# A second attention whose values run one pair later, whose pair shares a bank, and whose first scores move among the query panels

## What is computed

```python
s = jnp.einsum('bnqhgd,bnkhd->bnhgqk', qb, kw) * (HEAD_DIM_2 ** -0.5)
s = s - slopes[:, :, None, None] * dist.astype(jnp.float32)
s = jnp.where(mask[None, :, None, None], s, -jnp.inf)
m = jnp.maximum(jnp.max(s, axis=-1, keepdims=True), sink)
p = jnp.exp(s - m)
denom = jnp.sum(p, axis=-1, keepdims=True) + jnp.exp(sink - m)
o = jnp.einsum('bnhgqk,bnkhd->bnqhgd', p / denom, vw)
return o.reshape(B, T, ATTN_Q_DIM) @ w_out
```

## Time and profile before

| what | us |
|---|---|
| median of 3 runs | 2631.68 |
| lowest and highest | 2622.22, 2632.99 |
| the profiled execution's own time | 2619.79 |
| its span, first to last instruction | 2618.0 |
| TensorE matmuls busy in the span | 2490.8 (95%) |
| VectorE busy | 1694.2 (65%) |
| ScalarE busy | 931.9 (36%) |
| last query panel's last matmul to the first `SO` matmul (line 468) | 2096.98 to 2183.29 |

### The profile page before, as it was taken

The page is one execution under the profiler, slowest core; times in us unless marked ns, Lnnn a source line. Parts: engine busy times, 40 slices in busy tenths (PEclk is TensorE's granted clock), DMA queues, the critical chain, the costliest instruction groups (busy, mean ns, idle before and its releaser), DMA issues.

```text
span 2618.0 us, 34786 instructions
## 1 busy us (share of the span) xinstructions
PE 2490.8 (95%) x11828; PEld 2090.1 (80%) x11828; DVE 1694.2 (65%) x3166; ACT 931.9 (36%) x1315; POOL 739.6 (28%) x646
## 2 busy tenths in 40 slices
PE   8999999998999999999989899999999968999998
PEld 4877877686887887887778799999999746788786
DVE  5887768688666667676712377888888574444334
ACT  4223852623233333333222333333334473222222
POOL 0000000000025666676664256777730000000000
PEclk9999999998999999999999899999999988999999
DMA  6223813354234444444354489999996201222221
GB/s 248 97 73 116 311 48 121 115 190 153 81 125 141 137 141 137 148 142 137 129 184 158 159 290 329 364 365 362 360 366 217 89 9 57 89 96 96 88 96 64
DMA packets 177219, 433.56 MB, mean 166 GB/s; under 512 B 32752, under 2 KB 81904, under 8 KB 176752
## 3 DMA queue, kind: packets, MB, share of 16 engines
q1 hardware_dynamic: 123888, 331.61, 36.9%
q0 software_dynamic: 34816, 67.41, 7.3%
q10 hardware_dynamic: 18432, 33.56, 3.4%
HBM read 371.48 MB, written 61.01 MB: 165 GB/s over the span
## 4 chain that ended last, share of the span: by engine, by line
PE 82%; DVE 8%; ACT 4%; another core or an unknown queue 3%; issue 2%; ACTq 0%; DMA 0%; DVEq 0%; SPq 0%
PE ps L468 16%; PE ps L470 15%; PE ps L469 15%; PE ps L793 8%; PE ps L795 8%; PE ps L794 8%; DVE wlo L1372 2%; PE ps L706 2%; DVE ar L1425 1%; PE ps L690 1%; PE ps L538 1%; ACT whi L924 1%; PE ps L698 1%; ACT ar L1285 1%
## 5 line engine op out<-in xcount | busy, mean ns | idle before, releaser
L1372 DVE TENSOR_TENSOR wlo<-raw,whi 128x1024 fp32r<-128x1024 f32 x426 | 521.4, 1224 | 625.2 <-ACT whi L924 540.2
L2192 POOL DMA_INDIRECT w_scratch<-ar x384 | 416.8, 1085 | 986.6 <-DVE wlo L1372 881.0
L924 ACT ACTIVATE whi<-raw 128x1024 fp32r<-128x1024 f32 x424 | 448.9, 1059 | 687.6 <-PE ps L795 363.7
L468 PE MATMUL ps<-b_hi,whi 128*128 128x512 f32 x1328 | 524.4, 395 | 26.7 <-DVE wlo L1372 18.3
L470 PE MATMUL ps<-b_hi,wlo 128*128 128x512 f32 x1328 | 521.1, 392 | 0.2 <-issue 0.2
L469 PE MATMUL ps<-b_lo,whi 128*128 128x512 f32 x1328 | 521.2, 392 | 0.0
L793 PE MATMUL ps<-a_hi,whi 128*128 128x384 f32 x1024 | 347.6, 339 | 13.1 <-DVE a_lo L1949 11.0
L794 PE MATMUL ps<-a_lo,whi 128*128 128x384 f32 x1024 | 346.4, 338 | 0.4 <-issue 0.4
L795 PE MATMUL ps<-a_hi,wlo 128*128 128x384 f32 x1024 | 346.2, 338 | 0.4 <-issue 0.4
L468 PE MATMUL ps<-a_hi,whi 128*128 128x512 f32 x816 | 325.5, 399 | 8.9 <-DVE wlo L1372 7.2
L468 PEld LDWEIGHTS ps<-b_hi,whi 128*128 128x128 f32 x1328 | 251.7, 190 | 86.1 <-DVE wlo L1372 24.1
(11 more groups left out here) (273 smaller groups left out, 3039.1 us busy)
## 6 DMA issues: line engine op xcount, KB each, us to landing
raw<-panels SPq DMA_DIRECT2D x430, 512.0 KB
gelu_scratch<-ar ACTq DMA_DIRECT2D x128, 256.0 KB
w_scratch<-rstd SPq DMA_DIRECT2D x32, 768.0 KB, 11.1
ar<-w_scratch SPq DMA_DIRECT2D x128, 192.0 KB
ar<-gelu_scratch SPq DMA_DIRECT2D x128, 192.0 KB
ar<-mod SPq DMA_DIRECT2D x32, 512.0 KB, 5.2
ar<-panels SPq DMA_DIRECT2D x3, 2048.0 KB, 20.4
w_scratch<-ar POOLq DMA_INDIRECT x384
```

The source lines that it names most:

```text
L468: pe.matmul(bank, w_h, hi[:, k, :], start=(k == 0), stop=False)
L924: act.activation(whi[:, u % SPLIT, :], raw[:, u % RAW, :], ACT.Copy).then_inc(hi_ready, 1)
L1372: dve.tensor_tensor(wlo[:, u % SPLIT, :], raw[:, u % RAW, :], f32(whi[:, u % SPLIT, :]), ALU.subtract).then_inc(lo_ready, 1)
L2192: nc.gpsimd.indirect_dma_start(experts, bass.IndirectOffsetOnAxis(offs[:, k:k + 1], 0), vals[:, k:k + 1], None)\
```

## The change

- `swa_values(m)` is issued after the first transpose step of pair m + 1 and before its second. The last pair's values come after both of its own.
- A pair's two halves of the values go to one bank, 2 + m % 2, each on its own 64 partitions. `swa_hi` and `swa_lo` take a whole pair, 128 partitions at a time: 8 of each where there were 16.
- The banks change place: scores in 4 to 7, transposes in 0 and 1, values in 2 and 3.
- `swa_scores(0)` is issued after the sixth query panel. VectorE runs `swa_bias(0)` and `swa_bias(1)` after the seventh query panel, before the eighth.
- ScalarE's order for a pair is out, exp, hi, out, exp. VectorE's is norm, norm, bias, bias (of pair m + 2), lo.
- `s2` has 6 groups, `p2T` 3. `rstd1` and the bias tables are moved in the arena; `tiny` grows to 96 columns.
- The first `SO` panel waits for 7 of the 8 pairs, and for the eighth after its fourth step.

The core of the difference (swa_bias and swa_norm are the same but for `n % 6` and the banks):

```diff
-        s2 = area(A_S2, 4, 1024)
+        s2 = area(A_S2, 6, 1024)
-        p2T = area(A_PT2, 4, 512)
+        p2T = area(A_PT2, 6, 512)
...
             def swa_values(m):
...
                 pe.wait_ge(ptc2, 2 * m + 2)
-                if m:
-                    pe.wait_ge(o2, 2 * m)
-                else:
-                    pe.wait_ge(rt_ready, 5)
+                if m >= 2:
+                    pe.wait_ge(o2, m - 1)
                 for s in tiles:
                     for half in range(2):
                         rows_ = slice(half * HD2, (half + 1) * HD2)
                         kv = 2 * kt + half
-                        last = pe.matmul(ps[rows_, 6 + half, :], v2[:, b - 1 + s, kv * HD2:(kv + 1) * HD2], p2T[:, 2 * half + s, :],
+                        last = pe.matmul(ps[rows_, 2 + m % 2, :], v2[:, b - 1 + s, kv * HD2:(kv + 1) * HD2],
+                                         p2T[:, 2 * ((2 * m + half) % 3) + s, :],
                                          start=(s == tiles[0]), stop=(s == 1))
...
+            def early_scores(i, u):
...
+                if not (isinstance(i, int) and i == 0) and u == 1:
+                    pe.wait_ge(v2_done, 2)
+                    pe.wait_ge(rt_ready, 5)
+                    pe.wait_ge(bank_free, r_of(SW + 4) + 8)
+                    swa_scores(0)
+
+            strips(SW + 4, 8, a_hi, a_lo, early_scores, banks=SWB)
+            pe.wait_ge(bank_free, r_of(SO) + 4)
             swa_scores(1)
             for m in range(len(groups) // 2):
                 if m + 2 < len(groups) // 2:
                     swa_scores(m + 2)
                 swa_turn(2 * m)
+                if m:
+                    swa_values(m - 1)
                 swa_turn(2 * m + 1)
-                swa_values(m)
-
-            pe.wait_ge(o2, len(groups))
-            strips(SO, KT, b_hi, b_lo)
+            swa_values(len(groups) // 2 - 1)
+
+            def last_outputs(k):
+                if k == KT // 2 - 1:
+                    pe.wait_ge(o2, len(groups) // 2)
+
+            pe.wait_ge(o2, len(groups) // 2 - 1)
+            strips(SO, KT, b_hi, b_lo, each=last_outputs)
...
             swa_exp(0)
             swa_exp(1)
-            for n in range(0, len(groups), 2):
-                for c in range(2):
-                    if n + 2 < len(groups):
-                        swa_exp(n + 2 + c)
-                    if n:
-                        swa_hi(n - 2 + c)
-                swa_out(n)
-                swa_out(n + 1)
-            swa_hi(len(groups) - 2)
-            swa_hi(len(groups) - 1)
+            for m in range(len(groups) // 2):
+                more = 2 * m + 2 < len(groups)
+                swa_out(2 * m)
+                if more:
+                    swa_exp(2 * m + 2)
+                if m:
+                    swa_hi(m - 1)
+                swa_out(2 * m + 1)
+                if more:
+                    swa_exp(2 * m + 3)
+            swa_hi(len(groups) // 2 - 1)
...
+                if n == 6:
+                    dve.wait_ge(bias_ready, NH2 // 2)
+                    swa_bias(0)
+                    swa_bias(1)
+
             dve.wait_ge(bias_ready, NH2)
-            dve.wait_ge(bank_free, r_of(SO) + 4)
-            swa_bias(0)
-            swa_bias(1)
-            for n in range(0, len(groups), 2):
...
+            swa_bias(2)
+            swa_bias(3)
+            for m in range(len(groups) // 2):
+                swa_norm(2 * m)
+                swa_norm(2 * m + 1)
+                if m + 2 < len(groups) // 2:
+                    swa_bias(2 * m + 4)
+                    swa_bias(2 * m + 5)
+                if m:
+                    swa_lo(m - 1)
+            swa_lo(len(groups) // 2 - 1)
```

More of the change, by code:

```diff
@@ L496, in two_panels, with strips, four @@
                         tile(1, s - LAG)
-            def strips(first, count, hi, lo, after=None, ready=None, banks=(0, 1, 2, 3), two=False):
-                def four(i, ready=None):
+            def strips(first, count, hi, lo, after=None, ready=None, banks=(0, 1, 2, 3), two=False, each=None):
+                def four(i, ready=None, each=None):
                     for u in range(4):
                         if not (ready and two and u < 2):
-                            panel(i * 4 + (first + u), u, ps[:, banks[u], :], hi, lo, i * 4 + (r_of(first) + u + 1), ready if u == 0 else None)
+                            panel(i * 4 + (first + u), u, ps[:, banks[u], :], hi, lo, i * 4 + (r_of(first) + u + 1), ready if u == 0 else None,
+                                  each if u == 0 else None)
                         elif u == 0:
@@ L510, in four @@
                         after(i, 4)
-                four(0, ready)
+                four(0, ready, each)
                 if count > 4:
@@ L832, in _ @@
                 last.then_inc(v2_turned, 1)
[L833 to L842, removed]
             groups = [(b, kt, half) for b in range(TT) for kt in range(2) for half in range(2)]
@@ L865, in swa_turn @@
                     for r in range(4):
-                        last = pe.transpose(ps[:, 4 + s, r * P:(r + 1) * P], s2[:, n % 4, r * 256 + s * P:r * 256 + (s + 1) * P], ident)
+                        last = pe.transpose(ps[:, s, r * P:(r + 1) * P], s2[:, n % 6, r * 256 + s * P:r * 256 + (s + 1) * P], ident)
                 last.then_inc(pt2, 1)
@@ L2020, in _, with swa_bias @@
                 dve.tensor_copy(v2[:, :, u * P:(u + 1) * P], ps[:, 4 + u, :].rearrange("p (s n) -> p s n", n=P)).then_inc(v2_done, 1)
+            groups = [(b, kt, half) for b in range(TT) for kt in range(2) for half in range(2)]
+            def swa_bias(n):
+                b, kt, half = groups[n]
+                o = 16 * (n % 6)
+                dve.wait_ge(sc2, n // 2 + 1)
+                if n >= 6:
+                    dve.wait_ge(pt2, n - 5)
+                for r in range(4):
+                    h = 8 * kt + 4 * half + r
+                    at = P if b == 0 else 0
+                    dve.tensor_tensor_reduce(s2[:, n % 6, r * 256 + at:(r + 1) * 256],
+                                             ps[:, 4 + 2 * half + r // 2, (r % 2) * 256 + at:(r % 2) * 256 + 256],
+                                             bias[:, h, at:256], 1.0, -3.0e38, ALU.add, ALU.max, tiny[:, o + r:o + r + 1]).then_inc(bias2, 1)
+                dve.wait_ge(bias2, 4 * (n + 1))
+                h = 8 * kt + 4 * half
+                dve.tensor_tensor(tiny[:, o:o + 4], tiny[:, o:o + 4], col("sinks", h, 4), ALU.max).then_inc(mx2, 1)
+                dve.wait_ge(mx2, n + 1)
+                dve.tensor_scalar(tiny[:, o + 4:o + 8], tiny[:, o:o + 4], -1.0, None, ALU.mult).then_inc(nmx2, 1)
+                dve.tensor_tensor(tiny[:, o + 12:o + 16], col("sinks", h, 4), tiny[:, o:o + 4], ALU.subtract).then_inc(nmx2, 1)
@@ new lines, in swa_norm @@
+            def swa_norm(n):
+                o = 16 * (n % 6)
+                dve.wait_ge(e2, 4 * (n + 1))
+                dve.wait_ge(snk2, n + 1)
+                dve.tensor_tensor(tiny[:, o + 8:o + 12], tiny[:, o + 8:o + 12], tiny[:, o + 12:o + 16], ALU.add).then_inc(den2, 1)
+                dve.wait_ge(den2, n + 1)
+                dve.reciprocal(tiny[:, o + 12:o + 16], tiny[:, o + 8:o + 12]).then_inc(rec2, 1)
+                dve.wait_ge(rec2, n + 1)
+                at = P if groups[n][0] == 0 else 0
+                pr = s2[:, n % 6, :].rearrange("p (r n) -> p r n", r=4)[:, :, at:256]
+                dve.tensor_tensor(pr, pr, tiny[:, o + 12:o + 16].unsqueeze(2).to_broadcast([P, 4, 256 - at]), ALU.mult).then_inc(pn2, 1)
@@ L2021, in _, with swa_lo @@
+            def swa_lo(m):
+                b, kt, half = groups[2 * m]
+                dve.wait_ge(ohi2, m + 1)
+                at = slice(b * P, (b + 1) * P)
+                dve.tensor_tensor(b_lo[:, kt * 4:kt * 4 + 4, at], ps[:, 2 + m % 2, :].rearrange("p (r t) -> p r t", r=4),
+                                  f32(b_hi[:, kt * 4:kt * 4 + 4, at]), ALU.subtract).then_inc(o2, 1)
             for n in range(8):
```

88 lines of the change are left out of this document (19 added, 69 removed).

## The result

The changed kernel takes 2607.9 us (median of 4 runs, 2598.1 to 2610.7); the kernel before 2632.3 (4 runs, 2622.2 to 2634.8). The ratio is 0.9911 with a 95% interval of 0.9887 to 0.9934: 23 us less (24 by the medians), and between 17 and 30. A second set, taken with the experiments, gave 2607.1 against 2632.4, 0.9901 (0.9870 to 0.9933).

What follows compares the result with a forecast made beforehand. TensorE, with matmuls in 95% of the span, was taken as the bound, its idle time in second attention (85.9 us) the target. Pairs 11.0, head 1.9 and tail 2.1 sum to 15.0 us, giving 2616.7 us, range 2606 to 2627.

Steps and rivals of the forecast that it cites:

- The pairs: Second attention, first transpose of pair 0 to that of pair 7: 63.3 us falls to 52.3, gain 11.0.
- The loop of two pairs: Second attention, a loop through TensorE, ScalarE and VectorE: 15.95 us for two pairs, 8.0 a pair.
- The head: End of the query panels to the first transpose: 11.7 us falls to 9.8 at the lower clock, gain 1.9.
- the 8 to 10 that the prediction gave as a sign of being right: Second attention's start: first transpose 8 to 10 us after the last query panel.
- The cover over the early biases: VectorE before the eighth query panel ends: pair 0's biases and `wlo` fit, with 1.6 us of cover left.
- The tail: First transpose of pair 7 to the first output matmul: 11.0 us falls to 8.9, gain 2.1.
- The 1.5 us of the last hi and lo: First output panel: the eighth pair's hi and lo, 1.5 us, are hidden by 12 matmuls, some 2.7 us.
- it stays high throughout: TensorE's clock stays high in second attention: gain 11.0 + 3.7 + 3.7 = 18.4, time 2613.3; chance 0.16.
- The rival of halves in turn: Values in one bank no longer overlap, 3.9 us at the upper level: gain 9.7, time 2622.0; chance 0.10.
- The change of tiling: Values between transposes change TensorE's tiling each pair: counted 0; a drain would cost under 1 us on head and tail.

Runs made afterwards that it cites:

- The second trace: The changed kernel run once more with no further edit: 2607.1 us, 0.9901 of the kernel before; stage 70.1 us.
- the last run with idle matmuls: Changed kernel with VectorE's order norm, bias, norm, bias, lo and idle matmuls where TensorE waits for VectorE: 2604.3 us, 0.9901 of the kernel before.
- the split lo: Changed kernel with hi and lo again in two halves of 64 partitions: 2565.3 us, against 2577.3 before on that chip; stage 75.5 us.

## Why the prediction was right, and where not

**The pairs** came out at 52.5 against 52.3, and that this is so near is luck. Pair 0 took 7.5 and not 5.7: the first transposes of pair 1 are queued behind the scores of pair 3, which ran at the lower level, 3.79 in place of 2.0, and the prediction had priced pair 0 by VectorE alone. The other way, pair 6 has no biases left to add, and took 7.0 and not 8.0. The loop of two pairs, the mechanism of this part, held: 15.8 us from pair 3 to pair 5 and 15.6 from pair 4 to pair 6, reckoned 15.95. What did not hold is the premise that it takes the new place of the values to get there. One bank alone, on the old order, has periods of 8.3 where its values run at the upper level: ScalarE's hi waited for values of 3.5 us, not for their place. The prediction's rivals ask what the clock does to the new order; none asks what it does to the old one. That hi and lo cost the same on 128 partitions as on 64 was right too (0.58 and 0.69 us), and so was that VectorE is next to the bound.

**The head** gained 4.2 and not 1.9. I took the scores of pair 2 at the lower level, 3.8, since they had it before; they took 2.0, which is 1.8 of the difference; the rest are shorter waits. The 7.5 lie below the 8 to 10 that the prediction gave as a sign of being right. The cover over the early biases held, but narrowly: the `wlo` behind them started at 2106.74 and ended 0.3 before the panel did, where 1.6 was reckoned. The early scores run ahead of the seventh panel and push its end back too, by 1.3, and the prediction moved only the end of the eighth. Undone, the head costs 3.9.

**The tail** gained 4.0 and not 2.1: values of pair 6 took 1.94 and not 3.5. The 1.5 us of the last hi and lo are hidden as reckoned.

**The step that failed is the choice of the clock's level** for the scores of pair 2 and the values of pair 6. With both at the upper level the prediction had 18.4 us for the stage, as the rival "it stays high throughout"; measured are 18.9, with the clock at 0.92 and not high throughout. The second trace (70.1, a gain of 15.8) lies near the forecast's 15.0, by its sum and not by its parts: the head gained 4.2 there too, the pairs 9.3 and the tail 2.4. The rule that I used, that a step keeps the level at which it ran before, is no rule once the gaps ahead of it change.

**The bank.** The rival of halves in turn fell: no values step of one bank was longer than at two. In the last run with idle matmuls, two matmuls of full width and 512 columns (4 records) take 1.88 us at the upper level, and four of half width (8 records) 1.94: the halves overlap. The sentence of the Trainium skill's "PSUM — Partial Sum Buffer", section PSUM bank collisions raise a hardware error, that column tiles may write one bank on disjoint partitions at the same time, agrees with 1.94 us for 8 records.

**The change of tiling**, which the prediction counted as 0, left no gap to be seen: transposes from 2144.48 take 1.09, the values start at 2145.50 and take 1.94, and the next transposes start at 2147.37.

**The time.** The stage gives 16 to 19 us, the medians 24 and 25. The intervals (from 17) take in the 19; whether anything outside the stage was gained isn't settled. From the first output matmul to the end are 434.7 us before and 434.8 in the changed kernel. Ahead of the stage the traces differ by what the same code does from run to run, and the trace of before is of the shortest of its five executions, that of the changed kernel of the longest of its four. That the median lies 9 us below the forecast is thus explained by the stage for some 1 to 4 us only; the rest stays open.

## What to carry to other kernels

Before you reorder, price TensorE's steps at both levels of its clock, in the old order as well as in the new one. Here the wait that the new order was to remove was there because the values took 3.5 us in place of 1.94, and a cheaper step (one bank and one hi for a pair) had removed most of it. Take the parts of a change one by one on the kernel before: undone one by one on the changed kernel, the place of the values looked worth all 19 us, because ScalarE's new order needs it. Then find which engine is the bound next, since from there its instructions show, as the split lo did. And where one program's stage differs by 3 us between two traces, take a second trace before you read a difference of 2.

## What the runs showed of the hardware that I had not expected

- Idle matmuls make an unchanged order faster: the stage of the kernel before fell from 85.9 to 78.8 us with 24 more records, its granted clock rose from 0.80 to 0.91. In the kernel before, the values at 2147.51 ran at the lower level after a stretch in which TensorE had only the two transpose steps of their pair and waits.
- One bank for a pair took one hi off ScalarE, reckoned 5 us, and gave 10.9. With idle matmuls in both kernels it gave 5.9. So some 5 us seem to have come from the clock, which was granted at 0.91 in place of 0.80, as if the gain fed itself; one trace of each can't show that it always does.
- The same program had 67.0 and 70.1 us for the stage in two traces, by which steps fell to the lower level.
